# A mirrored Fourier transform, in one block with the gates and the output

## What is computed

```python
def fourier_mix(u, w_f):
    b, n, _ = u.shape
    ug = u.reshape(b, n, N_FOURIER_GROUPS, FOURIER_GROUP_W).astype(jnp.float32)
    z = jnp.fft.fft2(ug, axes=(1, 3), norm='ortho').real.astype(u.dtype)
    y = jnp.einsum('bngc,gcd->bngd', z, w_f)
    return y.reshape(b, n, FOURIER_W)

def gated_merge(p, attn_out, w_f, w_o):
    ga = p[..., GA0:F0]
    fu = p[..., F0:GF0]
    gf = p[..., GF0:D_IN]
    y = jnp.concatenate([attn_out * jax.nn.silu(ga), fourier_mix(fu, w_f) * jax.nn.silu(gf)], axis=-1)
    return y @ w_o
```

## Time and profile before

| | us |
|---|---|
| median of 3 runs | 1791.6 (1791.49 to 1797.52) |
| span of the profiled execution | 1794.3 |
| TensorE busy | 1661.6 (93%) |
| VectorE busy | 1014.5 (57%) |
| ScalarE busy | 832.4 (46%) |
| GpSimd busy | 505.2 (28%) |
| last gate tile drained | 1449.7 |
| first output matmul | 1602.0 |
| last output matmul handed on | 1786.7 |

### The profile page before, as it was taken

One profiled execution on the slowest core, in us unless ns is written; L12 is line 12 of the kernel. 1 busy time (PEld: TensorE's weight loads), 2 busy tenths in 40 slices (PEclk: granted clock), 3 DMA queues, 4 the chain that ended last, 5 costly groups with the idle time before them and its releaser, 6 DMA issues. The chain is left out here.

```text
span 1794.3 us, 22369 instructions
## 1 busy us (share of the span) xinstructions
PE 1661.6 (93%) x7388; PEld 1314.8 (73%) x7388; DVE 1014.5 (57%) x1451; ACT 832.4 (46%) x1042; POOL 505.2 (28%) x281
## 2 busy tenths in 40 slices
PE   7798885899999999999999999979999969988998
PEld 1487773677777777777777777768888848877886
DVE  1468776687787777778778778530000322254553
ACT  1454532466666766667666666711111132331111
POOL 0032332255445545545444544510000000000000
PEclk9799996799999999999999999989999979999999
DMA  6655445300000000000000000083231035658761
GB/s 223 250 179 169 158 144 133 128 15 23 21 23 16 21 23 15 24 22 15 23 21 16 22 21 23 6 223 124 105 117 47 28 145 199 188 163 231 215 219 74
DMA packets 120466, 171.01 MB, mean 95 GB/s; under 512 B 16065, under 2 KB 82625, under 8 KB 117858
## 3 DMA queue, kind: packets, MB, share of 16 engines
q1 hardware_dynamic: 111874, 147.30, 25.5%
q0 software_dynamic: 8544, 23.07, 4.0%
HBM read 119.89 MB, written 50.46 MB: 95 GB/s over the span
## 5 line engine op out<-in xcount | busy, mean ns | idle before, releaser
L826 DVE TENSOR_REDUCE chunk_max<-max_ps 128x1 f32<-128x512 f32 (+1 forms) x640 | 395.4, 635 | 66.3 <-PE max_ps L892 60.6
L755 POOL TENSOR_TENSOR prob_lo<-prob,prob_hi 128x1024 fp32r<-128x1024 f32 x128 | 306.5, 2395 | 417.3 <-ACT prob L788 417.3
L787 ACT ACTIVATE prob_hi<-s_ps 128x1024 fp32r<-128x1024 f32 x288 | 294.9, 1024 | 229.2 <-PE s_ps L910 229.1
L788 ACT ACTIVATE prob<-s_ps 128x1024 f32<-128x1024 f32 x288 | 293.6, 1019 | 0.0
L892 PE MATMUL max_ps<-k_hi,blk_q_hilo 128*128 128x512 f32 (+1 forms) x640 | 248.1, 390 | 30.3 <-DVE chunk_max L826 12.9
L909 PE MATMUL s_ps<-blk_q_hilo,k_hi 128*128 128x512 f32 x576 | 233.3, 405 | 1.1 <-DVE blk_q_negm L842 0.8
L910 PE MATMUL s_ps<-blk_q_negm,k_lo 65*128 65x512 f32 x576 | 229.3, 398 | 0.0
L930 PE MATMUL hi_ps<-prob_hi,v_hl 128*128 128x512 f32 x576 | 227.6, 395 | 1.5 <-POOL prob_lo L755 1.0
L932 PE MATMUL lo_ps<-prob_lo,v_one 128*128 128x512 f32 x576 | 228.6, 397 | 0.0
L931 PE MATMUL lo_ps<-prob_hi,zero_one 128*128 128x512 f32 x576 | 227.0, 394 | 0.0
L848 DVE TENSOR_TENSOR prob_lo<-prob,prob_hi 128x1024 fp32r<-128x1024 f32 x160 | 197.1, 1232 | 28.4 <-ACT prob L788 28.4
(11 more groups left out here) (169 smaller groups left out, 2508.0 us busy)
## 6 DMA issues: line engine op xcount, KB each, us to landing
tab<-in_dft POOLq DMA_DIRECT2D x16, 1024.0 KB, 7.1
w_mod<-in_w_mod SPq DMA_DIRECT2D x6, 2048.0 KB, 17.4
x<-in_x SPq DMA_DIRECT2D x8, 1024.0 KB, 5.5
h_scratch<-h_hi SPq DMA_DIRECT2D x8, 1024.0 KB, 4.2
h_scratch<-h_lo SPq DMA_DIRECT2D x8, 1024.0 KB, 6.5
q_scratch<-q_hilo SPq DMA_DIRECT2D x16, 512.0 KB, 3.2
blk_q_hilo<-q_scratch SPq DMA_DIRECT2D x32, 256.0 KB, 2.8
hh<-h_scratch SPq DMA_DIRECT2D x4, 2048.0 KB, 10.5
```

The source lines that it names most:

```text
L755: nc.gpsimd.tensor_tensor(prob_lo[slot3(j)][:], prob[slot3(j)][:], prob_hi[slot3(j)][:].bitcast(F32), ALU.subtract).then_inc(s_lo_pool, 1)
L787: nc.scalar.activation(prob_hi[slot3(j)][:], s[:], ACT.Exp)
L788: nc.scalar.activation(prob[slot3(j)][:], s[:], ACT.Exp).then_inc(s_exp, 1)
L826: last = nc.vector.reduce_max(chunk_max[:, qt, kc:kc + 1], bank[:, 0:MAX_CHUNKS[kc]], X_AXIS)
```

## The change

The three blocks become one, `tail`, with all SBUF buffers at fixed offsets, loops written out, and no barrier between the stages.

The transform uses that cosine is even and sine is odd about position 0 of each sequence. Of each of the sums (j = 0 and 2) positions m and 512-m are added and subtracted on VectorE: the first half of the folded sequence takes the sum (cosine rows), the second the difference (sine rows). For j = 1 and 3 two sequences are folded with each other's mirror image, which leaves cosines only; j = 3 is j = 1 with the sign of the sine part turned and the output written in reverse. So a step of the transform needs one table product per row where there were two. The m products give z (128 columns per even class, 256 for the odd classes together). Position 256 of j = 0 has no partner in the scheme and is added as a single row (`fold_mid`).

The folds use operands read backwards (`u3[:, g, :0:-1]`). They stand on VectorE in the last token group: two operations per channel group from its start, ten behind each u tile. GpSimd copies the edge elements. ScalarE rounds the four folded arrays between its tiles 5 and 6. There are 3 tables of 2 MB, 16 KB in a row per partition, where there were 16 of 1 MB.

y stays in SBUF (`y_half`); the output reads it there and there is no `y_scratch`. The loads of w_o follow the last z product.

```diff
+            for g in range(GROUPS):
+                dve.wait_ge(s_free, 2 * MT + g + 5)
+                nc.vector.tensor_tensor(f_w[:, g, :], u0[:, g, :], u2[:, g, :], ALU.add).then_inc(s_fold, 1)
+                dve.wait_ge(s_fold, PRE_STEPS * g + 1)
+                nc.vector.tensor_tensor(u2[:, g, :], u0[:, g, :], u2[:, g, :], ALU.subtract).then_inc(s_fold, 1)
+            for g in range(GROUPS):
+                done = GROUPS * PRE_STEPS + g * G_STEPS
+                dve.wait_ge(s_free, LAST + g + 5)
+                dve.wait_ge(s_fold, done)
+                nc.vector.tensor_tensor(f_t[:, g, :], u1[:, g, :], u3[:, g, :], ALU.add).then_inc(s_fold, 1)
...
+                nc.vector.tensor_tensor(f_t[:, g, 1:], u2[:, g, 1:], u3[:, g, :0:-1], ALU.subtract).then_inc(s_fold, 1)
+                nc.vector.tensor_tensor(f_w[:, g, 1:], u3[:, g, 1:], u2[:, g, :0:-1], ALU.add).then_inc(s_fold, 1)
+                nc.vector.tensor_tensor(f_s[:, g, 1:256], u0[:, g, 1:256], u0[:, g, :256:-1], ALU.add).then_inc(s_fold, 1)
...
+                    if tg == N_TG - 1 and n == 5:
+                        act.wait_ge(s_fold, FOLD_STEPS)
+                        act.wait_ge(s_edge, 1)
+                        nc.scalar.activation(mid_hi[:, :, 0:1], mid[:, :, 0:1], ACT.Copy).then_inc(s_chi, 1)
+                        for i in range(4):
+                            nc.scalar.activation(c_hi[i][:], folds[i][:], ACT.Copy).then_inc(s_chi, 1)
+            act.wait_ge(s_m, 2)
+            act.wait_ge(s_acc, LAST + 8)
+            for i, part in ((0, PLUS_MA), (1, PLUS_MB)):
+                nc.scalar.activation(m_hi[:, :, part, :], z_ps[i].rearrange("p (g c) -> p g c", g=GROUPS),
+                                     ACT.Copy).then_inc(s_mhi, 1)
...
+            pool.wait_ge(s_acc, LAST + 8)
+            pool.dma_start(tab[0][:], d["dft"][0]).then_inc(s_tab[0], 16)
+            pool.wait_ge(s_clo, 3)
+            pool.dma_start(tab[1][:], d["dft"][1]).then_inc(s_tab[1], 16)
+            pool.wait_ge(s_clo, 5)
+            pool.dma_start(tab[2][:], d["dft"][2]).then_inc(s_tab[2], 16)
...
+            def z_even(cls):
+                pe.wait_ge(s_clo, cls + 2)
+                for kt in range(SUBT):
...
+                    for g in range(GROUPS):
+                        out = z_ps[n % 4][:, g * P:(g + 1) * P]
+                        rows = slice(kt * P, (kt + 1) * P)
+                        hi, lo = c_hi[cls][:, g, rows], c_lo[cls][:, g, rows]
+                        m_h, m_l = m_rows(g, PLUS_MA if kt < 2 else PLUS_MB)
+                        nc.tensor.matmul(out, hi, m_h, start=True, stop=False)
+                        if cls == 0 and kt == 2:
+                            split_matmul(nc.tensor, out[0:1], mid_hi[:, g, 0:1], mid_lo[:, g, 0:1],
+                                         *m_rows(g, PLUS_MA), False, False)
+                        nc.tensor.matmul(out, hi, m_l, start=False, stop=False)
+                        last = nc.tensor.matmul(out, lo, m_h, start=False, stop=True)
+                    last.then_inc(s_z, 1)
+
+            def z_odd():
+                pe.wait_ge(s_clo, 5)
+                for i in range(2 * SUBT):
...
+                    for e in range(2):
...
+                        split_matmul(nc.tensor, out, c_hi[2][:, g, rows], c_lo[2][:, g, rows], *m_double(g), True, False)
+                        last = split_matmul(nc.tensor, out, c_hi[3][:, g, rows], c_lo[3][:, g, rows],
+                                            m_hi[:, g, 0:2, :], m_lo[:, g, 0:2, :], False, True)
+                    last.then_inc(s_z, 1)
+
+            def dft(step, cls, part, kt, g):
+                cols = slice(part * P, (part + 1) * P)
+                return split_matmul(nc.tensor, acc[g][:], z_hi[cls][:, kt, g, cols], z_lo[cls][:, kt, g, cols],
+                                    tab[cls][:, kt, 0, :], tab[cls][:, kt, 1, :], kt == 0, kt == SUBT - 1)
...
+            z_even(0)
+            z_even(1)
+            dft_rows(0, 0, 0)
+            z_odd()
+            dft_rows(1, 1, 0)
+            dft_rows(2, 2, 0)
             for g in range(GROUPS):
...
+                pe.wait_ge(s_y, 2 * GROUPS + g + 1)
+                for kt in range(SUBT):
+                    last = dft(3, 2, 1, kt, g)
+                last.then_inc(s_dft, 1)
```

More of the change, by code:

```diff
@@ L979, in project_gates @@
         NG = MT - GROUPS
+        LAST = (N_TG - 1) * MT
         w_raw = k.w_raw
[L981 to L987, removed]
@@ L989, in project_gates @@
+        acc = [ctx.enter_context(nc.psum_tensor(f"acc{i}", [P, TG], F32)) for i in range(GROUPS)]
+        o_ps = [ctx.enter_context(nc.psum_tensor(f"o_ps{i}", [P, 2, 512], F32)) for i in range(2)]
+        z_ps = [o_ps[i // 2][:, i % 2, :] for i in range(4)]
         S = k.sem
@@ L998, in project_gates @@
         den_rows = [v.rearrange("b (a q) -> (b a) q", q=P) for v in (k.den_dram, k.inv_dram)]
[L1000 to L1003, removed]
+        x_v = d["x"][0].rearrange("(t p) n -> t p n", p=P)
+        out_v = d["out"][0].rearrange("(t p) n -> t p n", p=P)
+        w_o_v = d["w_o"][0].rearrange("(a k p) n -> a p k n", a=2, p=P)
+        PRE_STEPS, G_STEPS = 2, 10
+        FOLD_STEPS = GROUPS * (PRE_STEPS + G_STEPS)
+        Z_TILES = 4 * SUBT
         block = ctx.enter_context(nc.Block())
@@ L1059, in _ @@
+            for i in range(3):
+                pool.wait_ge(s_tab[i], 16)
+            pool.wait_ge(s_half, 1)
+            for t in range(TT):
+                e = t % 2
+                pool.wait_ge(s_mean, t + 1)
+                nc.gpsimd.tensor_tensor(rstd[e][:], mean[e][:], minus_half[:], ALU.pow).then_inc(s_rstd, 1)
         @block.scalar
@@ L1063, in _ @@
                 act.sem_inc(s_st[i], 16)
-            def body(tg, slot, i):
+            for tg in range(N_TG):
                 for n in range(MT):
@@ new lines, in y_out @@
+            def y_out(step, g):
+                act.wait_ge(s_dft, step * GROUPS + g + 1)
+                out = y[g][:, ::-1, 3] if CLASSES[step] == 3 else y[g][:, :, CLASSES[step]]
+                nc.scalar.activation(out, acc[g][:], ACT.Copy).then_inc(s_y, 1)
+            for n in range(2 * SUBT):
+                z_high(n)
+            for i in range(GROUPS):
+                y_out(0, i)
+                z_high(2 * SUBT + 2 * i)
+                z_high(2 * SUBT + 2 * i + 1)
+            for g in range(GROUPS):
+                y_out(1, g)
@@ new lines, in _, with m_rows, m_double @@
+                    if tg == N_TG - 1 and n == 9:
+                        pe.wait_ge(s_in, 32)
+                        for i in range(2):
+                            nc.tensor.matmul(z_ps[i], chan[:, i, :], wf[:].rearrange("p g c -> p (g c)"), start=True,
+                                             stop=True).then_inc(s_m, 1)
+            pe.wait_ge(s_mlo, 3)
+            def m_rows(g, part):
+                return m_hi[:, g, part, :], m_lo[:, g, part, :]
+            def m_double(g):
+                return (m_hi[:, g, PLUS_MA:PLUS_MA + 1, :].broadcast_to([P, 2, P]),
+                        m_lo[:, g, PLUS_MA:PLUS_MA + 1, :].broadcast_to([P, 2, P]))
```

732 lines of the change are left out of this document (328 added, 404 removed).

## The result

The changed kernel takes 1740.8 us (median; 1739.1 to 1742.8), the kernel before 1793.9 us beside it (1791.5 to 1797.5). The ratio is 0.970, with a 95% interval of 0.968 to 0.972: 53 us less, where I had forecast 1711 us, 1698 to 1732. The direction is right; 30 us of the saving are missing and the time lies outside the range. The profiled execution has a span of 1741.0 us.

What follows compares the result with a forecast made beforehand. The last stretch was taken as bound by TensorE's number of matmuls. Its terms summed to 256.4 us against 337.0, 80.6 less, so the 1794.3 us span becomes 1713.7; less 2.7 for the median, 1711 us, range 1698 to 1732.

Steps and rivals of the forecast that it cites:

- The break before z: Between the last gate drain and z, TensorE idles for two copies and three subtractions in a chain: 3.4 us.
- The price of a narrow product at full clock: 128-column matmuls for z's even classes: 0.10 us each, 10.8 us for 108, ends 7.6 and 26.
- The folds: VectorE's folds beside the last gate tiles end near 1414.5 if reversed operands stream like straight ones; nothing is paid.
- the fourth rival: Slower than before: costly reversed folds exhaust 12 us of cover and stop TensorE at tile ten; chance 0.03.
- the first: Rival: narrow matmuls of z lose their single pass, 0.24 us each, 15 us more, 1726 us; chance 0.33.
- The third: Rival: attention inputs land last, output starts some 6 us later, 1717 us; chance inside the main forecast's 0.45.
- the clock in the narrow products: In z's even classes after the break, 2 us were added to the 10.8 us for the low clock.
- wf: Ahead of the channel product TensorE waits 2 to 6.5 us for this small weight: 5 taken, plus 1 for clock.
- I count 1 us: Break before output group 2: inputs there at 47, prepared at 55.5, TensorE done with the first group at 56.
- Eight output groups are 768 x 0.227: The output keeps its 768 wide matmuls at 0.227 us each: 174.4 us.
- Three small stalls at once: Remaining case of several small stalls at once, ending in the 1730s; chance 0.05.
- The second rival: All small terms go well: wf in time, clock kept, 0.07 us per narrow matmul, no output wait; 1698 us, chance 0.14.

Runs made afterwards that it cites:

- kernel 2: Changed kernel with the channel matrices split behind gate tile nine instead of behind the last drain: 1726.0 us, ratio 0.962 to the kernel before.
- Kernel 3: Changed kernel with the 96 narrow products of z's even classes streaming 256 columns instead of 128, result wrong: 1731.9 us, one run.
- kernel 1: Changed kernel with the first table load issued only when chan and wf have landed: 1728.4 us, ratio 0.963 to the kernel before.
- 7: Changed kernel with each table sent as four loads, in pieces of 4 KB per partition instead of 16 KB: 1733.4 us, one run.
- the kernel without waits: Changed kernel with tables behind wf, early channel split, buffers on multiples of 128, second group's inputs early, attention remainder behind w_o's first remainder row: 1699.5 us, ratio 0.946.
- kernel 5: Changed kernel with the buffers from 163808 up starting 96 bytes lower, on multiples of 128: 1732.5 us, ratio 0.967 to the kernel before.
- 4: Changed kernel with the buffers from 163808 up starting 32 bytes lower, on multiples of 64: 1738.7 us, ratio 0.968 to the kernel before.

## Why the prediction was wrong, step by step

**Right.** The matmuls taken out: the transform's steps run at 0.227 us per matmul where the addresses allow, 10.9 us for 48, and z of the odd classes took 11.4 us. The break before z (3.4, measured 3.5). The price of a narrow product at full clock: 0.10 taken, 0.11 measured, 11.4 us for the 108 where the sum had 10.8. (The 81 ns of the Trainium skill, "TensorE: Matmul & The Clock Gate", section "Back-to-back issue gap", would have given 8.7; the 0.11 us measured in kernel 2 decides.) The folds: the last ended at 1415.4 (1414.5 predicted, before a shift of 3.2 us), the edges at 1416.3, and the reversed operands cost what straight ones do (groups of VectorE's lines between 1384 and 1416 us in the changed kernel, with busy us and mean ns of one):

```profile
L1292 DVE TENSOR_TENSOR u_even<-fold_w,fold_t 128x512 f32<-128x512 f32 x4 | 2.8, 691 | 0.1
L1295 DVE TENSOR_TENSOR fold_t<-u_even,u_odd 128x511 f32<-128x511 f32 x4 | 2.8, 692 | 0.1
L1296 DVE TENSOR_TENSOR fold_w<-u_odd,u_even 128x511 f32<-128x511 f32 x4 | 2.7, 682 | 0.0
```

ScalarE drained tile six at 1428.2, well ahead of tile ten, so the fourth rival was nothing, nor was the first: at full clock no pass was lost. The fourth rival had a slip in it: the 24 reversed folds cover 8168 elements per partition (two of 511 and four of 255 in each of four groups) and not 6128, so they would have had to cost some 2.4 times a straight one, not 2.9, to use up the 12 us; they cost 1.0. The third did not occur: the attention inputs were there at 1535.8, 20.6 us after the last odd product (20 predicted). The remainder of y was ready at 34.5 (34.2 predicted).

**Wrong 1, the clock in the narrow products: 9.0 us, and 1.0 in the step behind them.** The sum had "(10.8 + 2)", 2 us for the low clock. The price of a product was right and the clock term was wrong by a factor of five. I carried over from the earlier trace rows that the clock comes back soon after a break; those rows show 256-column matmuls. Kernel 3 shows that with that width it would have come back here too, kernel 2 that without the break nothing is lost. The range of the narrow price reached to 26 us, so the measured 21.8 lie inside it, but for another reason, and its condition, the break, was a part of the kernel that I had counted at 3.4 us.

**Wrong 2, wf: 5.7 us.** "nothing if it is served quickly. I take 5, and 1 us for the clock". TensorE waited 9.1. The rule that I had put beside it, of the Trainium skill ("DMA: Bandwidth & Descriptors", section "Queues, rings and completion order"), is that an engine takes the queues' rows in turn, a packet at a time, and I had worked out from it that larger pieces would bring the wait to its upper end. The trace agrees (98 pieces against 99), and so do kernels 1 and 7 (3.4, 12.3 and 18.4 us with no tables, 4 KB pieces and 16 KB pieces); I took a middle value all the same. The upper end, 6.5 us, was too low too: it had the tables alone at 422 GB/s, while they shared the engines with SyncE's queue and took 17 us, not 15. And an idle stretch of 9 us has its clock behind it: the channel product at 3.8 us instead of 1.9, the next tiles 0.7 us more.

**Wrong 3, the output: 5.2 us in groups 2 to 8, 2.5 in the break before them, and 0.7 in the transform.** The break ("I count 1 us") had its terms nearly right, inputs at 51 instead of 47 us, but I asked when the inputs are prepared, and TensorE waited for the drain of a bank that stands behind that preparation on VectorE: the sum itself takes 1.2 us more, and 3.4 us of low clock follow, 1.7 of the 5.2. The rest, 3.5, is the address: "Eight output groups are 768 x 0.227" took the price from a kernel whose output and transform ran at 0.227; the change put the second copy of y, two of the three tables and half of w_o's remainder off a multiple of 128. (Where they lay before is not on record, only that their matmuls came 0.2267 apart.) Nothing in the earlier trace rows shows that a place can matter; the rows of the gates did, in the kernel before, where token groups 1 and 3 ran at 0.233 and groups 2 and 4, but for their first tiles, at 0.227, and only the end of group 4 had been read.

**Three small stalls at once** had 0.05 in my chances, "in the 1730s". It was what happened, only larger: the stalls summed to 1740.8, outside the range. The misses were not independent: a wait, then the clock on it, then work too narrow to win the clock back. The second rival, in which all small terms go well, was set at 1698 us; the kernel without waits takes 1699.5. That is in part chance: 4.4 us of it come from the gates' buffers, which the rival left alone, and its narrow products at 0.07 us are 0.11.

## What to carry to other kernels

Ask of every break ahead of TensorE what runs behind it: here 3.5 us of idle time ahead of 128-column matmuls cost 14.9 us; ahead of 256-column ones the clock was back after 2.9 us. Issue a small load that someone waits for ahead of large ones, or cut the large ones into small pieces. And when a change moves matmul operands, look at their byte offsets: where a stream's starts are 2 or 3% further apart than elsewhere with nothing waited for, start the buffers on multiples of 128.

## What was unexpected in the hardware

- 128-column reduced-precision matmuls came 0.213 us apart at the low clock, as far as 256-column ones, and 0.11 us at the full one, near the 0.12 of 256 columns. Half the columns gave hardly any time back at either level. The weight load takes 0.33 us there at the low clock and 0.19 at the full, and overlaps; why 128 columns are hardly cheaper was not tried.
- A stream of 108 of them kept the full clock over 11.4 us but did not regain it in 21.8 us, with TensorE busy all the time.
- The break before output group 2 left the granted clock at 1.00 where it was 1.8 us (kernels 2 and 7) and 2.2 us (kernel 5); it fell to 0.50 at 2.3 us (kernel 1) and at 3.2 to 3.5 us (the changed kernel, 3, 4).
- Start offsets off a multiple of 128 bytes cost 3.3 or 6.7 ns per matmul of 512 columns (0.2300, 0.2333 against 0.2267 us). That both operands count is seen from the streams in which only one is off; by what mechanism is open.
- Reversed operands of VectorE cost what straight ones do: 0.69 us for 511 elements.
